# MLA's next head projected between a head's last tiles, and GLA's next level-0 differences taken ahead of the normalization

## The reference

```python
q, k, v, g, a_lr = split(x @ w_in)
log_a = log_sigmoid(a_lr @ w_a2 + b_a2) / 16
b = cumsum(log_a)                       # within a chunk
att[i, j] = sum_d q[i, d] k[j, d] exp(b[i, d] - b[j, d])      # j <= i
o = att @ v + (q * exp(b)) @ state
state = exp(b_last) * state + (k * exp(b_last - b))^T @ v
o = o * rsqrt(mean(o * o) + 1e-5) * norm_g
y = (o * silu(g)) @ w_out
```

```python
q_a, c_kv, k_pe, z = split(h @ w_in)                 # 384, 256, 64, 1024 wide
q = rmsnorm(q_a) @ w_q_b                             # per head 128 + 64 (rotated)
kv = rmsnorm(c_kv) @ w_kv_b                          # per head k 128, v 128
sc = (q_nope @ k_nope^T + rope(q_pe) @ rope(k_pe)^T) * scale
o = softmax(sc) @ v
y = (o * silu(z)) @ w_out
```

## Time and profile before

| | |
|---|---|
| median of 3 runs | 3131.76 us (3129.99 to 3139.81) |
| the profiled execution | 3129.38 us, its span 3127.5 us |
| mean granted PE clock | 0.962 of full speed |
| busy share of the span | PE 90%, PEld 74%, DVE 49%, ACT 38%, POOL 31% |
| GLA | from about 55 us to 530 us of the span |
| MLA's input, gate slots | about 2430 us to 2525 us |
| MLA, pair projections to last tile | about 2533 us to 3016 us |

### The profile page before, as it was taken

The page is one execution under the profiler, slowest core; times in us unless marked ns, Lnnn a source line. Parts: engine busy times, 40 slices in busy tenths (PEclk is TensorE's granted clock), DMA queues, the critical chain, the costliest instruction groups (busy, mean ns, idle before and its releaser), DMA issues. The chain is left out here.

```text
span 3127.5 us, 38981 instructions
## 1 busy us (share of the span) xinstructions
PE 2829.2 (90%) x14702; PEld 2313.1 (74%) x14702; DVE 1546.4 (49%) x1992; ACT 1186.9 (38%) x1974; POOL 962.4 (31%) x490
## 2 busy tenths in 40 slices
PE   6989887989999999979699999999699979999888
PEld 5777775868888888867377777777586757878776
DVE  5765756632444144466546656566631234444353
ACT  4122123232444234442445555555522234344331
POOL 3542543234344443422143333333022230000020
PEclk9999998989999999989799999999899989999999
DMA  4213321311001110013110111111131100000021
GB/s 150 87 54 107 108 93 48 120 58 44 28 29 34 34 42 27 27 52 107 46 54 28 41 42 34 35 41 41 40 116 41 40 34 14 7 14 7 7 87 54
DMA packets 57288, 162.06 MB, mean 52 GB/s; under 512 B 8400, under 2 KB 10064, under 8 KB 57168
## 3 DMA queue, kind: packets, MB, share of 16 engines
q1 hardware_dynamic: 49968, 134.17, 12.9%
q10 hardware_dynamic: 7200, 26.22, 2.4%
HBM read 133.99 MB, written 17.99 MB: 49 GB/s over the span
## 5 line engine op out<-in xcount | busy, mean ns | idle before, releaser
L108 POOL TENSOR_SCALAR w_hi<-w_raw 128x1024 fp32r<-128x1024 f32 x126 | 141.3, 1122 | 1573.9 <-PE at L134 385.7
L110 POOL TENSOR_TENSOR w_lo<-w_raw,w_hi 128x1024 fp32r<-128x1024 f32 x126 | 306.8, 2435 | 19.0 <-issue 5.2
L1256 PE MATMUL pj<-x_hi,w_hi 128*128 128x512 f32 x688 | 285.9, 416 | 4.9 <-ACT swa_swapped L1387 4.9
L132 PE MATMUL pj<-x_hi,w_hi 128*128 128x512 f32 x636 | 258.7, 407 | 33.9 <-DVE mla_q_pe L2254 12.2
L1258 PE MATMUL pj<-x_hi,w_lo 128*128 128x512 f32 x688 | 270.7, 393 | 0.0
L1257 PE MATMUL pj<-x_lo,w_hi 128*128 128x512 f32 x688 | 270.6, 393 | 0.0
L134 PE MATMUL pj<-x_hi,w_lo 128*128 128x512 f32 x636 | 251.4, 395 | 0.0
L133 PE MATMUL pj<-x_lo,w_hi 128*128 128x512 f32 x636 | 251.4, 395 | 0.0
L1707 PE MATMUL pj<-x_hi,w_hi 128*128 128x512 f32 x496 | 216.4, 436 | 7.1 <-ACT da_raw L1822 7.1
L1709 PE MATMUL pj<-x_hi,w_lo 128*128 128x512 f32 x496 | 195.7, 395 | 0.0
L1708 PE MATMUL pj<-x_lo,w_hi 128*128 128x512 f32 x496 | 195.0, 393 | 0.0
(11 more groups left out here) (347 smaller groups left out, 6468.7 us busy)
## 6 DMA issues: line engine op xcount, KB each, us to landing
w_raw<-w_slots SPq DMA_DIRECT2D x158, 512.0 KB, 3.2
o_t<-ada_t ACTq DMA_DIRECT2D x24, 512.0 KB, 3.3
ada_row<-ada_t ACTq DMA_DIRECT2D x24, 512.0 KB, 3.4
x_res<-o_t SPq DMA_DIRECT2D x24, 512.0 KB, 2.7
o_t<-x_res SPq DMA_DIRECT2D x24, 512.0 KB, 7.8
da_swapped<-da_raw SPq DMA_DIRECT2D x64, 128.0 KB, 2.3
o_t<-x_t SPq DMA_DIRECT2D x4, 1024.0 KB, 9.0
o_t<-x_t SPq DMA_DIRECT2D x8, 512.0 KB, 7.6
```

Source lines behind the costliest of these rows:

```text
L110: nc.gpsimd.tensor_tensor(g.w_lo[:, u, :], g.w_raw[:, u, :], g.w_hi[:, u, :], ALU.subtract)\
L132: nc.tensor.matmul(dst, w_hi, x_hi[:, k, cols], start=(j == 0), stop=False)
L1256: nc.tensor.matmul(proj(half), g.w_hi[:, u, w], g.x_hi[:, k, cols[half]], start=(k == 0), stop=False)
```

## The change

Four things in GLA. PE now does both halves of the next head's k projection before the matmuls of the squares (`ms_done`). DVE takes `sub(0)` of the next head before it waits for the reciprocal root, into `decayed_k_t`, which is free since its transpose. ACT copies the next q, exponentiates level 0 and copies the next k before it waits for the squares' sum. POOL makes the level-0 operand before it splits the fourth slot (the second of v's weights in the buffer order), and waits for `ms_done` before it, since the squares lie in the same buffer.

In MLA's input the latents lie in `o_t[3:8]`, their high and low parts in buffers of their own (`lat_hi`, `lat_lo`), and are made before the gate slots' work instead of behind it; PE no longer waits for the key's bank before the first gate slot but before the second.

In MLA the rounded q parts of all heads are made while the pairs are rotated (`split_pair`, `lower_pair`); q is projected into `at[0:S]`, k into `at[S:2S]`, v into `pj[0]`. The projections of the next head stand between the last tiles of a head: q ahead of the product of tile 6, k ahead of the product of tile 7, v behind it. The loop has three passes and the last two heads stand behind it.

```diff
 # gla_phase, PE
                 if not last:
                     start_slot(h + 1, 1)
                     half(1, 0)
+                    half(1, 1)
                 pe.wait_ge(m.sq_ready, h + 1)
 ...
                 mm.then_inc(m.ms_done, 1)
-                if not last:
-                    half(1, 1)
-
+
+            pe.sem_inc(m.ms_done, 1)
 # ACT
+                def enter(h):
+
+                    act.wait_ge(g.slot_done, h * 6 + (s0 + 1))
+                    nc.scalar.activation(q_t[:, :], g.pj[:, 0, :], ACT.Copy, scale=GLA_DK ** -0.5).then_inc(m.act_evac, 1)
+                    level_exp(0, h)
+                    act.wait_ge(g.slot_done, h * 6 + (s0 + 2))
+                    nc.scalar.copy(k_t[:, :], g.pj[:, 1, :]).then_inc(m.act_evac, 1)
 ...
                 act.drain()
+                act.sem_inc(m.head_end, 1)
                 nc.scalar.activation(mm_in[:, :, :], dd[:, :, :], ACT.Square).then_inc(m.sq_ready, 1)
-                act.wait_ge(m.ms_done, h + 1)
+                if h < GLA_HEADS - 1:
+                    enter(h + 1)
+                act.wait_ge(m.ms_done, h + 2)
 # POOL
                 split_slot(nc, pool, g, base, h * 6)
+                pool.wait_ge(m.act_evac, h * 4 + 2)
+                level_operand(0)
                 split_slot(nc, pool, g, base + 1, h * 6)
-                pool.wait_ge(m.act_evac, h * 4 + 2)
-                for n in range(3):
+                for n in range(1, 3):
 # DVE
-                sub(0)
+                if h == 0:
+                    sub(0)
                 sub(1)
 ...
+                if h < GLA_HEADS - 1:
+                    dve.wait_ge(m.kd_done, h + 1)
+                    sub(0, g.b[:, h + 1:h + 2, :])
                 dve.wait_ge(m.rs_ready, h + 1)
 # mla_in_phase, PE, ACT, DVE
             pe.wait_ge(m.evac, N_L)
-            pe.wait_ge(m.swapped, 1)
-            pe.wait_ge(m.cosined, 1)
 ...
+            for l in range(N_L):
+                act.wait_ge(m.normed, l + 1)
+                nc.scalar.copy(g.lat_hi[:, l, :], raw[:, l, :]).then_inc(m.hi_ready, 1)
             with act.Fori(0, KT // 2) as i:
 ...
+            for l in range(N_L):
+                dve.wait_ge(m.hi_ready, l + 1)
+                nc.vector.tensor_tensor(g.lat_lo[:, l, :], raw[:, l, :], g.lat_hi[:, l, :], ALU.subtract)
             with dve.Fori(0, KT // 2) as i:
 # mla_phase, PE: head(i, u, last), new
+                scores(0)
+                turn_v()
+                scores(1)
+                turn_p(0)
+                for n in range(2, NT):
+                    scores(n)
+                    output(n - 2)
+                    turn_p(n - 1)
+                if not last:
+                    pe.wait_ge(g.w_ready, h + (s0 + 4))
+                    pe.wait_ge(m.exps, h * NT + (NT - 1))
+                    project_q(1 - u)
+                output(NT - 2)
+                turn_p(NT - 1)
+                if not last:
+                    pe.wait_ge(m.exps, h * NT + NT)
+                    project_k(1 - u)
+                output(NT - 1)
+                if not last:
+                    project_v(1 - u)
 # ACT, the pairs and a head
+                if j >= 2:
+                    split_pair(j - 2)
                 swap_halves(nc, swp[:, j % 2, :], pe_banks[j]).then_inc(m.swapped, 1)
+            split_pair(2)
+            split_pair(3)
 ...
+                    elif not last:
+                        take_q(h + 1)
 ...
+                if not last:
+                    take_kv(h + 1)
 # DVE, the pairs and a head
+                if j >= 2:
+                    lower_pair(j - 2)
                 dve.wait_ge(m.swapped, j + 1)
 ...
+                if not last:
+                    lower_q(h + 1)
+                    lower_k(h + 1)
                 dve.wait_ge(m.pv_done, h * NT + NT)
```

More of the change, by code:

```diff
@@ L2126, in mla_phase, with heads @@
         at = g.at
+        cols = (slice(0, HALF), slice(HALF, S))
+        q_bank, k_bank, v_bank, out = at[:, 0:S], at[:, S:2 * S], g.pj[:, 0, :], g.pj[:, 1, :]
         pe_banks = (g.pj[:, 0, :], g.pj[:, 1, :], at[:, 0:S], at[:, S:2 * S])
+        def heads(engine, head):
+            with engine.Fori(0, PAIRS - 1) as i:
+                head(i, 0, False)
+                head(i, 1, False)
+            head(PAIRS - 1, 0, False)
+            head(PAIRS - 1, 1, True)
         @block.sync
@@ new lines, in turn_p, with output @@
+                def turn_p(n):
+                    pe.wait_ge(m.p_ready, h * NT + (n + 1))
+                    if n == 0:
+                        pe.wait_ge(m.v_ready, h + 1)
+                    else:
+                        pe.wait_ge(m.pt_evac, h * NT + n)
+                    for t in range(NT):
+                        mm = nc.tensor.transpose(g.pj[:, 0, t * P:(t + 1) * P], p[:, n % 2, t * P:(t + 1) * P], g.ident[:, :])
+                    mm.then_inc(m.t_done, 1)
+                def output(n):
+                    pe.wait_ge(m.pt_evac, h * NT + (n + 1))
+                    if n == 0:
+                        pe.wait_ge(m.o_taken, h + 1)
+                    for t in range(NT):
+                        mm = nc.tensor.matmul(out[:, n * P:(n + 1) * P], v[:, t, :], pt[:, n % 2, t * P:(t + 1) * P],
+                                              start=(t == 0), stop=(t == NT - 1))
+                    mm.then_inc(m.pv_done, 1)
@@ L2208, in _, with split_pair @@
+                output(NT - 1)
+                if not last:
+                    project_v(1 - u)
+            for h in range(MLA_HEADS):
+                head(h // 2, h % 2, h == MLA_HEADS - 1)
         @block.scalar
         def _(act):
-            act.sem_inc(m.pt_evac, 1)
+            def split_pair(j):
+                act.wait_ge(m.pe_ready, j + 1)
+                for c in range(2):
+                    hi = nc.scalar.copy(pe_both[own[c], 2 * j + c, :], q_pe[own[c], j % 2, :])
+                hi.then_inc(m.pe_hi_ready, 1)
@@ L2249, in _ @@
+            take_q(0)
+            take_kv(0)
+            heads(act, head)
         @block.vector
@@ L2291, in drain_stream @@
+            lower_q(0)
+            lower_k(0)
+            heads(dve, head)
 def drain_stream(nc, g, name):
@@ L2353, in build @@
         g.k_pe_hi, g.k_pe_lo = sb("mla_k_pe_hi", [P, S], F32R), sb("mla_k_pe_lo", [P, S], F32R)
-        mla_in_phase(nc, g)
-        mla_phase(nc, g)
+        with ExitStack() as mla:
+            g.lat_hi, g.lat_lo = (mla.enter_context(nc.sbuf_tensor(n, [P, 5, S], F32R)) for n in ("mla_latents_hi", "mla_latents_lo"))
+            mla_in_phase(nc, g)
+            mla_phase(nc, g)
         if stop == "mla":
```

265 lines of the change are left out of this document (120 added, 145 removed).

## The result

The changed kernel takes 3098.74 us (median of 4 runs, 3094.95 to 3104.03); the kernel before, beside it, 3135.78 (4 runs). The ratio is 0.9889, 95% interval 0.9870 to 0.9907: faster by 1.1%. The forecast was 3070.5 with a range to 3086, so the time lies 28 us above the forecast and outside the range. The profiled execution took 3094.95 us, span 3093.1, against 3129.38 and 3127.5: 34.4 us less where the sum promised 61.1.

A forecast was written before the change was run, and what follows sets the result against it. PE was busy for 90% of the span, so only its waits and half clock could be won: 15.5 + 12.3 + 33.3 = 61.1 off 3129.4 gives 3068.3, plus 2.4 to the median 3070.7, stated as 3070.5; range 3059 to 3086.

The forecast's parts named there:

- MLA's heads, 33.3 us: Seven passages between MLA heads: filled ACT-copy waits and v's transposes moved gain 4.76 us each, 33.3 in all, bounds 19 and 39.
- C: Rival in MLA's heads: last tiles are not free for projections, a passage gains 2.7 us, time 3085; chance 0.11.
- D: Rival in MLA's heads: denser PE is granted 1.2 GHz, so slower, near 3450 with all heads so; chance 0.02.
- GLA, 15.5 us: Three passages between GLA heads gain 16.5 us without the level-0 wait, head 0 loses 1.0: 15.5, bounds 12 and 27.
- So the passage gains 4.6 to 5.5: GLA, per passage between heads: gain with level 1's operand at the late end (9 at the early end); 5.5 us taken.
- Rival B: GLA: the wait only moves from level 0 to level 1; GLA gives -1 us, time 3087; chance 0.11.
- an extra of 2.88 us: GLA's normalization: DVE's L677 takes 5.24 us beside POOL's split instead of 2.36 uncontended, 2.88 more.
- The rule that I had set beside rival B: GLA: the port lock makes DVE late by one POOL instruction, 2.39 us, not 2.88; 1.4 less in all.
- MLA's input and start, 12.3 us: MLA's input: first pair projection 11.3 us earlier, 1.0 of slow clock saved, rotation 0; 12.3 in all, bounds 9 and 15.
- the rotation's chain: MLA's start, from POOL's split to the first scores: 33.6 us as now despite new ACT and DVE work; gain 0, bounds -2 and +2.
- Slot 2's wait: MLA's input: gate slot 2 waits 1.3 us for DVE's first gate pass, which stands behind five low-part passes.
- the barrier: MLA's input, from gates to pair projections: one tanh and one gate pass make the first pair projection start 2.8 us later.

## Why the prediction was wrong

**MLA's heads, 33.3 us: right**, in mechanism and size (33.7 by the stage, 7 x 4.95 = 34.6 from exponential to exponential). The rivals C and D fell: no passage gained only 2.7, and from 2577.8 to 2983 the granted clock in after is 1.00.

**GLA, 15.5 us: wrong; 0.9 by the stage, 4.1 by three heads (and some 2.5 ahead of the stage, in head 0).** No wait before level 0, a wait of 4.04 us before level 1 at half clock (forecast 3 to 6), level 3 earlier by 5.5: all this came. The failing step is the one behind it, "So the passage gains 4.6 to 5.5": I followed the passage up to level 3 and POOL's operand of level 2, and took it that a gain there is kept until the next head. I didn't ask which engine the rest of the levels hangs on, though the trace of before has TensorE waiting 1.49 us for VectorE at level 5, behind 15.0 us of VectorE without a pause, and 36.3 us of waits for GpSimd. Rival B had the sign right (GLA gives nothing), but its place wrong: it put the wait at level 1, and it was at level 5. At 0.11 it weighed too little.

The working that was missing needs only VectorE's timeline of before. From the start of the normalization (182.66) to the end of level 4's accumulation (241.70) are 59.0 us, and in them VectorE waited three times, 5.04, 2.92 and 1.67 us, each time for TensorE's levels: 9.6 us of slack. The change starts the normalization 5.5 us later (forecast 5.0), takes `sub(0)` with its 1.3 us out of the stretch, and can take away no more than the slack; so VectorE is done 5.4 us earlier at best (9.6 + 1.3 - 5.5), whatever TensorE does. In after it is busy for 50.2 of the 51.0 us from 184.65 to 235.65, with one pause of 0.76: the slack is used up, and the bound of these levels is now VectorE. The 2.6 us left at level 5 are those 5.4 less that pause and 2.1 us of longer passes (50.2 us busy, where before had 49.4 with `sub(0)` in it); half clock behind the new wait takes 1.6 more.

The second failing step is the way I priced contention: as an extra of 2.88 us on passes that fall on a split, once, in the normalization. The rows show two engines in turn, so each of GpSimd's passes may delay VectorE anywhere in the levels, and the kernels with work left out confirm it in rough size: taking out of after the dot products, of which 25 of 1.21 us (30.3) lie between normalization and level 6 in three heads, saves 23.8 us; taking out the low parts, of which 12 of 2.4 us (28.8) lie there, saves 30.6, half clock behind waits included. The rule that I had set beside rival B, the lock of the shared port pair for a whole instruction (the Trainium skill, "SBUF — State Buffer", section "Terms"), agrees with the rows, where each pass waits for the end of the other engine's; I had applied it to one collision and not to the sum.

**MLA's input and start, 12.3 us: 5.3.** The mechanism (no waits for the key's bank and for the rounding) came, and the rotation's chain came at its forecast 33.6 us. Three sizes were off. Slot 2's wait was 1.3 in the sum and is 3.75, since the normalization of the last two latents fell beside a split (4.63 us for 2.48): the same miss as in GLA. The slow clock behind it was counted as nothing and costs 1.6 (5.59 us at 0.71); moving the gate pass gave back 4.6 to 5.6 for the two together. And the barrier: 2.8 in the sum, 4.79 measured, because GpSimd's last split ends behind VectorE's gate pass. The three make 6.0 of the 7.0 us missed. The last is read from the trace and was not tried.

**The base.** I took the profiled run as 2.4 us below the median of three runs. Over 35 runs of before in these comparisons the median is 3135.6, so the profile was 6 us lucky, most of it between GLA and MLA. It accounts for no more than a fifth of the miss.

## What to carry to other kernels

When a wait is removed, follow the gain to the end of the loop body: list for each later step which engine it came last from, and whether that engine paused since. Where VectorE and GpSimd both work out of SBUF, add their passes up as one queue and set that sum beside TensorE's time; if it is the larger, an earlier start of TensorE gives little (here 4.1 us of 16.5), and side work that stands ahead of the pass that TensorE waits for has to move behind it: here two dot products, worth 13.6 us with the restructuring and 4.5 without it. At a barrier, look at the last pass of every engine, not of the one you edit.

## What the runs showed of the hardware

In the rows of after from 223.73 to 233.51, passes of VectorE and GpSimd with both inputs in SBUF took turns to within 0.15 us, the listed time of the later one holding its wait (1.21 us became 2.5 to 3.4); passes of VectorE that read PSUM kept 1.21 us, and ScalarE's kept 1.0.

The same stage behind the same wait ran at half the granted clock in one execution and at the full one in another. In the kernel with only the gate pass moved, the last state stage of GLA, whose code and order are those of after, ran 11 us longer; windows of that kernel and of after over the same 122 operations (length, busy of PE, PEld, DVE, ACT, POOL, granted clock, DMA share, GB/s):

```profile
490.00:519.50 29.50, 29.38 (x122) 23.31 (x122) 7.46 (x16) 2.60 (x7) 1.75 (x1) 0.53 0.05 18
```

```profile
490.00:508.50 18.50, 18.13 (x122) 13.87 (x122) 7.69 (x16) 2.80 (x8) 1.98 (x1) 1.00 0.11 29
```

Both follow a wait of 1.14 us. These 11 us are most of the 15.5 that the change was to have in GLA, and a reason to compare stages over several profiles.
